# Experts of a mixture in plain fp32, weights stationary, instead of three reduced-precision products with the tokens stationary

## The reference, cut to what matters

```
logits = h @ w_router + b_router                 # 8 experts
probs  = softmax(logits); the two largest of each token are kept and normalised: gates
for e in range(8):
    y += gates[:, e] * ((silu(h @ w_gate[e]) * (h @ w_up[e])) @ w_down[e])
h = layer_norm(alpha * h + y)
```

## Time and profile before

| | us |
|---|---|
| median of 3 runs | 3124.86 (3122.19 to 3125.25) |
| the profiled execution's own time | 3119.76 |
| its span | 3117.9 |
| TensorE busy | 2736.0 (88%) |
| its weight loads busy | 2260.0 (72%) |
| VectorE busy | 2104.4 (67%) |
| ScalarE busy | 1550.2 (50%) |

### The profile page before, as it was taken

How to read it: one execution, slowest core, us unless ns; L and a number is a source line. 1 busy time by engine, 2 the same in 40 slices (tenths; PEclk the granted TensorE clock), 3 DMA queues, 4 the chain that set the end, 5 groups by cost and what they waited for, 6 DMA issues and landing times.

```text
span 3117.9 us, 50172 instructions
## 1 busy us (share of the span) xinstructions
PE 2736.0 (88%) x21428; PEld 2260.0 (72%) x21428; DVE 2104.4 (67%) x2999; ACT 1550.2 (50%) x2209; POOL 79.9 (3%) x93
## 2 busy tenths in 40 slices
PE   8787996759878799999999999997699988899987
PEld 8457996559866567676766667675697988897977
DVE  4655546784434588797979778796585865576864
ACT  4433432522111477676767667674336454446443
POOL 0000000030000000000000000000000011000011
PEclk9669997879987799898989899999799999999999
DMA  6113543200011798898979789895343454344542
GB/s 215 44 38 112 176 149 94 69 1 4 4 38 30 256 338 310 289 355 290 351 276 365 275 320 322 296 353 175 84 140 109 129 161 144 102 121 123 155 126 90
DMA packets 373442, 547.71 MB, mean 176 GB/s; under 512 B 24492, under 2 KB 187784, under 8 KB 372956
## 3 DMA queue, kind: packets, MB, share of 16 engines
q1 hardware_dynamic: 371228, 541.54, 51.2%
q0 software_dynamic: 1984, 2.89, 0.3%
HBM read 540.46 MB, written 1.05 MB: 174 GB/s over the span
## 4 chain that ended last, share of the span: by engine, by line
PE 71%; DVE 16%; ACT 6%; issue 3%; DMA 2%; POOL 1%; SPq 0%; DVEq 0%; POOLq 0%; ACTq 0%
PE PS L157 18%; PE PS L158 18%; PE PS L159 18%; DVE wl L304 4%; ACT wh L295 3%; PE PS L958 1%; PE PS L1689 1%; PE PS L372 1%; DMA raw<-in_w_in 1%; PE PS L1708 1%; PE PS L477 1%; PE PS L1716 1%; PE PS L986 1%; PE PS L2211 1%; PE PS L2183 1%
## 5 line engine op out<-in xcount | busy, mean ns | idle before, releaser
L304 DVE TENSOR_TENSOR wl<-raw,wh 128x1024 fp32r<-128x1024 f32 (+1 forms) x654 | 774.2, 1189 | 487.0 <-ACT wh L295 469.8
L295 ACT ACTIVATE wh<-raw 128x1024 fp32r<-128x1024 f32 (+1 forms) x654 | 670.6, 1027 | 669.9 <-PE PS L159 577.9
L304 DVE TENSOR_TENSOR wl<-more,wh 128x1024 fp32r<-128x1024 f32 x384 | 467.5, 1224 | 55.4 <-ACT wh L295 33.4
L295 ACT ACTIVATE wh<-more 128x1024 fp32r<-128x1024 f32 x384 | 406.8, 1060 | 141.9 <-PE PS L159 141.8
L157 PE MATMUL PS<-b_hn_h,wh 128*128 128x256 f32 (+2 forms) x1312 | 378.7, 289 | 26.3 <-DVE wl L304 10.8
L159 PE MATMUL PS<-b_hn_h,wl 128*128 128x256 f32 (+2 forms) x1312 | 371.1, 283 | 0.0
L158 PE MATMUL PS<-b_hn_l,wh 128*128 128x256 f32 (+2 forms) x1312 | 370.7, 283 | 0.0
L157 PE MATMUL PS<-wh,xe_h 128*96 128x512 f32 x896 | 358.0, 400 | 0.0
L158 PE MATMUL PS<-wl,xe_h 128*96 128x512 f32 x896 | 354.0, 395 | 0.0
L159 PE MATMUL PS<-wh,xe_l 128*96 128x512 f32 x896 | 351.1, 392 | 0.0
L157 PEld LDWEIGHTS PS<-b_hn_h,wh 128*128 128x128 f32 (+2 forms) x1312 | 232.1, 177 | 32.0 <-issue 16.9
(11 more groups left out here) (488 smaller groups left out, 5335.3 us busy)
## 6 DMA issues: line engine op xcount, KB each, us to landing
more<-in_moe_w_up SPq DMA_DIRECT2D x64, 1024.0 KB, 5.7
more<-in_moe_w_gate SPq DMA_DIRECT2D x64, 1024.0 KB, 5.5
more<-in_moe_w_down SPq DMA_DIRECT2D x64, 1024.0 KB, 5.5
raw<-in_w_in SPq DMA_DIRECT2D x56, 1024.0 KB
raw<-in_moe_w_gate SPq DMA_DIRECT2D x48, 1024.0 KB, 5.7
raw<-in_moe_w_up SPq DMA_DIRECT2D x48, 1024.0 KB, 5.3
raw<-in_moe_w_down SPq DMA_DIRECT2D x48, 1024.0 KB, 5.8
raw<-in_w_in SPq DMA_DIRECT2D x32, 704.0 KB
```

The source lines that it names most:

```text
L295: act.e.activation(st.two(n)[0], st.raw(n), ACT.Copy).then_inc(*act.sig("hi", st.name, n, sem=f"hi_{st.name}"))
L304: dve.e.tensor_tensor(lo, st.raw(n), hi.bitcast(F32), SUB).then_inc(*dve.sig("lo", st.name, n, sem=f"lo_{st.name}"))
```

## The change

- The three fp32r products and the split of the weights go. Each 128 x 128 tile of weights, as it was loaded, is the stationary operand of one plain fp32 matmul, and the 96 tokens of the expert move (`xe`, 128 x 96 for each of 8 feature tiles). The result has the hidden feature on the partitions, so `turned` goes too; the down product's result is transposed once (`turn`, 8 transposes an expert), scaled by the gate, split, and scattered with two fp32r products.
- The gather makes the transposed tokens directly (24 plain fp32 matmuls an expert, `Ht` stationary, `P1` moving); the picks of all experts are made at once, and the gates by slot by 24 small matmuls once.
- The weights lie in memory in the order in which the kernel reads them (`expert_tiles`, made before the launch): each load is 1 MB in one piece, 8 KB for each partition. Both sides read the same loads. A load is freed by the last matmul that uses it.
- There are 13 slots: six of them (EARLY) lie in memory that the layer before no longer uses from y_mean on, and SyncE issues six loads there right after the first three that follow bonus_v, ahead of the rest of rw_w_o and the router; three (RAW) and four (LATE, where wh and wl were) are used once the router's weights have been read. SyncE no longer waits for the flag.
- The high and low split of the transposed H goes; the rank is stored as rank + 1, and 0 for a token that isn't the expert's.

The diff, cut to its core (the dense side, which follows the same loads, and the constants are left out):

```diff
+    EARLY_AT = [u_at(3), u_at(5)] + [u_at(10) + n * 8192 for n in range(4)]
+    EARLY = [m_tile(f"early{n}", o, 2048) for n, o in enumerate(EARLY_AT)]
+    LATE = [m_tile(f"late{n}", PARTS_AT + n * 8192, 2048) for n in range(NPART)]
+    SM = Stream("M", EARLY + RAW + LATE, PARTS)
...
-    Ht = two("Ht", 3, D)
-    xe = [two(f"xe{n}", KC, CAP) for n in range(2)]
-    P1 = [tile3(f"P1{n}", 3, CAP, F32R) for n in range(2)]
-    G = tile("G", D)
-    PG = [tile(f"PG{n}", T) for n in range(2)]
-    hid = [tile(f"hid{n}", 512) for n in range(2)]
-    mh = two("mh", FE // 128, CAP)
...
+    Ht = tile3("Ht", 3, D)
+    P1 = tile("P1", 3 * NE * CAP).rearrange("p (i e r) -> p i e r", i=3, e=NE)
+    xe = [tile3(f"xe{n}", KC, CAP) for n in range(2)]
+    mt = [tile(f"mt{n}", 4 * CAP) for n in range(2)]
+    assert top[0] <= u_at(10)
+    top[0] = u_at(0)
+    mh = tile3("mh", NF, CAP)
+    Yh, Yl = tile("Yh", D, F32R), tile("Yl", D, F32R)
...
+            for j in range(2):
+                for x in range(2):
+                    SM.add(("in", e_, 2 * g + x, j), [(lambda sl: sl, A["moe_in"][e_, 2 * g + x, j])])
+        for n in range(KC * NF // 16):
+            SM.add(("out", e_, n), [(lambda sl: sl, A["moe_out"][e_, n])])
...
+    def load_moe(sp):
+        m = sp.piece["M"]
+        if m == 0:
+            sp.wait_ge(sp.at("y_mean"))
+        elif m == len(EARLY):
+            sp.wait_ge(sp.at("direct", "A", SA.of["router"]))
+        load(sp, SM)
...
+    def sparse_order(x, gather, project, down, turn, scatter):
+
+        gather(x, 0)
+        for e_ in range(NE):
+            project(x, e_, 0)
+            if e_:
+                turn(x, e_ - 1, 1)
+            project(x, e_, 1)
+            if e_:
+                scatter(x, e_ - 1)
+            for g in range(2, NG):
+                project(x, e_, g)
+            down(x, e_, range(0, 2))
+            if e_ + 1 < NE:
+                gather(x, e_ + 1)
+            down(x, e_, range(2, 6))
+            turn(x, e_, 0)
+            down(x, e_, range(6, 8))
+        turn(x, NE - 1, 1)
+        scatter(x, NE - 1)
...
     def sparse_pe(pe):
+        def gather(pe, e_):
+            pe.wait_ge(pe.at("picks"))
             for hf in range(2):
                 pe.wait_ge(pe.at("ht", 2, 1))
+                b = take("xe", e_, hf)
+                for k in range(4):
+                    f = 4 * hf + k
+                    for i, (q0, qn) in enumerate(QT):
+                        t = e.matmul(PS[:, b, k * CAP:(k + 1) * CAP], Ht[0:qn, i, f * 128:(f + 1) * 128], P1[0:qn, i, e_, :],
+                                     start=i == 0, stop=i == 2)
                 t.then_inc(*pe.sig("xe_mm", e_, hf))
             rows_pe(pe, "rank_row", e_, rt)
+            if e_ == 0:
+                b = take("slots")
+                for x in range(NE):
+                    for i, (q0, qn) in enumerate(QT):
+                        t = e.matmul(PS[0:CAP, b, x:x + 1], P1[0:qn, i, x, :], sc[i][0:qn, 56 + x:57 + x], start=i == 0,
+                                     stop=i == 2)
+                t.then_inc(*pe.sig("slots_mm"))
+
+        def project(pe, e_, g):
+            for j, what in enumerate(("gate", "up")):
+                pe.wait_ge(pe.at("xe", e_, 1))
+                b = take(what, "s", e_, g)
+                for x in range(2):
+                    m = SM.of["in", e_, 2 * g + x, j]
+                    w = pair_view(moe_load(pe, m))
+                    for y in range(2):
+                        o = (2 * x + y) * CAP
+                        for k in range(KC):
+                            t = e.matmul(PS[:, b, o:o + CAP], w[:, y, k, :], xe[e_ % 2][:, k, :], start=k == 0, stop=k == KC - 1)
+                    t.then_inc(*moe_used(pe, m))
+                pe.also(what + ".mm", "s", e_, g)
+
+        def down(pe, e_, rows):
+            for i in rows:
+                if i % 4 == 0:
+                    take("yt", e_, i // 4)
+                o = i % 4 * CAP
+                for f in range(NF):
+                    c = i * NF + f
+                    m = SM.of["out", e_, c // 16]
+                    w = row_view(moe_load(pe, m))
+                    pe.wait_ge(pe.at("up", "s", e_, f // 4))
+                    t = e.matmul(PS[:, bank_of["yt", e_, i // 4], o:o + CAP], w[:, c % 16, :], mh[:, f, :], start=f == 0,
+                                 stop=f == NF - 1)
+                    if c % 16 == 15:
+                        t.then_inc(*moe_used(pe, m))
+                if i % 4 == 3:
+                    pe.also("yt.mm", e_, i // 4)
+
+        def turn(pe, e_, half):
+            pe.wait_ge(pe.at("yt", e_, half))
+            b = take("y", e_, half)
+            for i in range(4):
+                o = (4 * half + i) * CAP
+                t = e.transpose(PS[0:CAP, b, i * 128:(i + 1) * 128], YT[:, o:o + CAP], ident)
+            t.then_inc(*pe.sig("turn_mm", e_, half))
+
+        def scatter(pe, e_):
             pe.wait_ge(pe.at("rank_row", "s", e_))
             for f in range(KC):
+                pe.wait_ge(pe.at("y_lo", e_, f // 4))
+                b = take("scattered", e_, f)
+                c = slice(f * 128, (f + 1) * 128)
+                e.matmul(PS[:, b, 0:T], Yh[:, c], PG[e_ % 2], start=True, stop=False)
+                e.matmul(PS[:, b, 0:T], Yl[:, c], PG[e_ % 2], start=False, stop=True).then_inc(*pe.sig("scattered_mm", e_, f))
+
+        sparse_order(pe, gather, project, down, turn, scatter)
...
-                    for k1 in range(0, KC, 2):
-                        n, (wh, wl) = piece(pe, SM)
-                        for k in range(2):
-                            t = mm3(e, PS[0:CAP, b, :], xh[:, k1 + k, :], xl[:, k1 + k, :], wh[:, k, :], wl[:, k, :],
-                                    k1 + k == 0, k1 + k == KC - 1)
-                        t.then_inc(*used(pe, SM, n))
...
     def sparse_act(act):
+        def project(act, e_, g):
+            act.wait_ge(act.at("gate.mm", "s", e_, g))
+            if g >= 2:
+                act.wait_ge(act.at("up", "s", e_, g - 2))
+            elif e_:
+                act.wait_ge(act.at("up", "s", e_ - 1, NG - 1 if g % 2 == (NG - 1) % 2 else NG - 2))
+            e.activation(mt[g % 2], ps("gate", "s", e_, g, n=4 * CAP), ACT.Silu).then_inc(*act.sig("gate", "s", e_, g))
+
+        def turn(act, e_, half):
+            act.wait_ge(act.at("turn_mm", e_, half))
+            act.wait_ge(act.at("slots"))
             if e_:
+                act.wait_ge(act.at("scattered_mm", e_ - 1, KC - 1))
+            e.activation(Yh[0:CAP, half * 512:(half + 1) * 512], ps("y", e_, half, p=CAP, n=512), ACT.Copy,
+                         scale=gs[0:CAP, e_:e_ + 1]).then_inc(*act.sig("y_hi", e_, half))
...
     def sparse_dve(dve):
+        def project(dve, e_, g):
+            dve.wait_ge(dve.at("gate", "s", e_, g))
+            dve.wait_ge(dve.at("up.mm", "s", e_, g))
+            if e_:
+                dve.wait_ge(dve.at("yt.mm", e_ - 1, 1))
+            e.tensor_tensor(flat(mh[:, 4 * g:4 * g + 4, :]), mt[g % 2], ps("up", "s", e_, g, n=4 * CAP), MUL).then_inc(
+                *dve.sig("up", "s", e_, g))
+
+        def down(dve, e_, rows):
+            if rows[0] == 0:
+                return
+            half = 0 if rows[0] == 2 else 1
+            dve.wait_ge(dve.at("yt.mm", e_, half))
+            if e_:
+                dve.wait_ge(dve.at("turn_mm", e_ - 1, half))
+            e.tensor_copy(YT[:, half * 4 * CAP:(half + 1) * 4 * CAP], ps("yt", e_, half, n=4 * CAP)).then_inc(
+                *dve.sig("yt", e_, half))
+
+        def turn(dve, e_, half):
+            dve.wait_ge(dve.at("y_hi", e_, half))
+            c = slice(half * 512, (half + 1) * 512)
+            e.scalar_tensor_tensor(Yl[0:CAP, c], ps("y", e_, half, p=CAP, n=512), gs[0:CAP, e_:e_ + 1],
+                                   Yh[0:CAP, c].bitcast(F32), MUL, SUB).then_inc(*dve.sig("y_lo", e_, half))
+            dve.also("y", e_, half)
...
+        e.memset(Yh[CAP:128].bitcast(F32), 0.0)
+        e.memset(Yl[CAP:128].bitcast(F32), 0.0)
+        for i, (q0, qn) in enumerate(QT):
+            t = e.tensor_tensor(P1[0:qn, i], bc(iota_r[0:qn], [qn, NE, CAP], 1), bc(rk[i][0:qn], [qn, NE, CAP], 2), ALU.is_equal)
+        t.then_inc(*dve.sig("picks"))
+        sparse_order(dve, gather, project, down, turn, scatter)
...
-            for hf in range(2):
-                c = slice(hf * 512, (hf + 1) * 512)
-                dve.wait_ge(dve.at("ht_hi", i, hf))
-                e.tensor_tensor(Ht[1][0:qn, i, c], ps("ht", i, hf, p=qn, n=512), Ht[0][0:qn, i, c].bitcast(F32), SUB).then_inc(
-                    *dve.sig("ht", i, hf))
-        for i, (q0, qn) in enumerate(QT):
             dve.wait_ge(dve.at("rank_mm", i))
-            e.tensor_copy(rk[i][0:qn], ps("rank", i, p=qn, n=8)).then_inc(*dve.sig("rank", i))
+            e.scalar_tensor_tensor(rk[i][0:qn], ps("rank", i, p=qn, n=8), 1.0, mk[i][0:qn], ADD, MUL).then_inc(
+                *dve.sig("rank", i))
```

(54 more changed lines are left out.)

266 lines of the change are left out of this document (74 added, 192 removed).

## The result

The changed kernel takes 3289.23 us (median of 4 runs, 3285.77 to 3291.14), the kernel before 3123.53 beside it (3120.52 to 3125.25). The ratio is 1.0527, 95% interval 1.0514 to 1.054: slower by 165.7 us. Predicted were 3285 us, between 3238 and 3315, and slower with 0.93. The profiled execution took 3289.37, its span is 3287.4.

The account below looks back on a forecast made before the run. TensorE was taken to bound the experts' stage. 1046 + 1204 + 41 + 7 + 14 + 7.2 = 2319 for its end, 162 us later than 2156.87; so 3282 profiled, 3285 predicted, range 3238 to 3315.

Parts of the forecast that it names:

- The price of a pass: Main matmuls: each plain fp32 pass costs its weight load of 128 columns, 0.112 us; 10752 passes, 1204 us against 927.
- Rival (a): Main matmuls: loads hide and the moving side bounds, 0.081 us a pass, 871 us, total 2952, faster; 5 in 100.
- From the first main pass to the last: Experts' stage: main passes 1204 us, seven more gathers 41, turns 7, scatters 14.
- The start: Experts' stage up to its first main pass: that pass at about 1046 instead of 1054.49, 8.5 us gained.
- The branch: Ahead of the experts' memsets and picks: 3.5 us for the branch, on the other engines too.
- the slots' matmuls: 24 small matmuls for the gates by slot, before the first main pass: 4.0 to 7.8 us, taken as 4.5.
- The tail: End of the experts' stage, from the last pass through scatter and adds: 7.2 us, where it was 5.3.
- The splits are worth nothing by themselves: Experts' stage: the weight splits are off the path, so removing them gains nothing by itself.
- The loads hide: Expert weight loads: 44.04 MB an expert in about 159 us, 277 GB/s, stay hidden; 0 us added.
- The clock: TensorE in the experts' stage: granted clock near 1.00 where it was 0.94, since the seam no longer idles.
- rival (b): TensorE's clock falls to 0.50 for the whole experts' stage, 4414, or only at each expert's seam, 3353; 5 in 100.

## Why the prediction was right, step by step

**The price of a pass** was the step that decided, and it was exact: 0.112 predicted; measured 0.1115 in the last 112 passes, and the same within 0.001 in every group of one expert's window. The rows that it came from were a handful of loads elsewhere in the kernel. The runs with 64, 48 and 128 columns show that it is the load's and not the moving side's: it falls with the columns loaded, and at a given clock it stays when those moved are halved or grow by a third. Rival (a), the four matmuls of line 1716, showed a true spacing (0.084 where the load is short), of the side that does not bound.

**From the first main pass to the last**: predicted 1204 + 41 + 7 + 14 = 1266 us; measured 1057.28 to 2323.33, 1266.0. That the two agree so closely is partly chance: at the 0.1117 that is the mean of one expert's window the passes come to 1201, 3 less than 1204, and small things not in the sum (17 passes at half clock, gathers of 6.0) make up for it.

**The start** was mis-sized: 1046 predicted (the terms themselves add up to 1045.4), 1057.28 measured, 11.3 us, where the range allowed 5. 2.6 of it is where the stage began; executions with the same code ahead of it differ by 6.2 there (1008.67 and 1014.86, above), so this is no effect of the change that a run shows. The branch took 6.75 (0.55 + 0.10 + 6.10) where I had 3.5, because of the loads that the change itself puts beside it (3.48 for the 6.10 where they are held back). The gather took 10.55 where I had 8, the rank row 1.20 for 0.5, the slots' matmuls 7.77 for 4.5: all three ran at clock 0.50 to their end, the upper ends of the bounds given (10.4 and 7.8), where I had chosen the middle for the gather and a value near full clock for the slots' matmuls. The memsets, 2.0, and the picks, 2.7, were right. So the 8.5 us that the start was to gain came to nothing (46.3 for 46.1).

**The tail** took 5.8, not 7.2. After the stage the changed kernel needs 958.3 us, the one before 961.0; I had assumed them equal. With the same code there, the runs on the changed kernel lie between 956.4 and 961.0 and those on the kernel before between 961.0 and 965.1; why is not shown. The errors (+11.3, -1.4, -2.7) leave 3289.3 for the profiled execution against 3282. That the median came within 4 us of 3285 is partly luck: errors of opposite sign, and 3 us added for a distance between median and profiled execution that the changed kernel does not have (3289.23 and 3289.37).

**The splits are worth nothing by themselves**: right inside the stage, not at its start. In the kernel with the gather alone VectorE still makes them all, at 113.92 of 129.60 us, and TensorE is busy for 129.36. But the first high part and two low parts (1.07 and 2.36 us) stand ahead of the picks in the chain there, and putting the picks first was worth 11.4 us.

**The loads hide**: right, 278 GB/s; the DMA share in an expert is 0.81, just above the 0.8 that was named as its bound. No run shows a cost or a gain of the early loads. The layout, priced at zero, measured 1.0002.

**What the prediction did not split**: it set 927 us of main products against 1204, as one price. The runs divide it, in this order: the new gather -65, plain fp32 in place of three fp32r products +208, all the rest of the change +22, together +165 of the 165.7. Inside the stage (from the router's first matmul to the layer norm's adds) the same steps are -68.6, +209.1 and +29.1 in the profiled executions; the time outside it varies by 8 us between them, so the last step is known to some 7 us only. An expert's products take 168 x 0.69 = 115.9 us in three fp32r matmuls, 168 x 0.858 = 144.1 in plain fp32 with the tokens stationary, and 1344 x 0.1115 = 149.9 with the weights stationary; over eight experts that is 226 for the first step and 46 for the second. The first earns 11 back at the start (46.2 to 35.0). The second earns part of it back in each expert: the period grows by 2.3 us (156.8 to 159.1) instead of 5.8, since the hidden part needs no transposes (28 in each expert with the tokens stationary, 2.3 us) and the scatter uses fp32r (2.05 us for 3.67). That makes 18 us for the swap of sides over eight experts; the other 11 of the 29.1 are the longer start (35.0 to 46.3).

**The clock**: "I expect the opposite" was right for the stage (1.00 where it was 0.94), but the argument against rival (b) was thinner than its 5 in 100 suggests. It rested on 8 columns moved against 96; the run with 48 shows the fall of clock half way between, and its 4409 us are what rival (b) had priced (4414).

## What to carry to other kernels

Price a matmul by the larger of its two sides, at its own pass count: columns loaded and columns moved, each from a row of the same clock. Taking work off an engine that does not bound (here 105 us of VectorE in each expert) buys nothing where the two run side by side, and what it adds to TensorE's passes is paid in full; look in the profile at the busy time of weight loads beside that of matmuls. A change of many parts can hold a good one: test them one by one before dropping the whole.

## What the runs showed of the hardware

- Plain fp32 takes two passes whichever side is stationary: 0.429 us a pass with 512 columns moving, 0.1115 with 128 loaded and 96 or 128 moving, 0.083 to 0.084 with 64 loaded and 96 moving.
- A TensorE that is busy all the time can still be granted clock 0.50: with 128 columns loaded and 48 moved it stayed there for most of some 2400 us, and came back to 1.00 for moments behind matmuls of 272 columns.
- A branch costs 3.1 to 3.5 us until VectorE's first instruction with idle DMA engines, and 5.6 to 6.5 where weight loads fill them (six runs; holding the loads back took it from 6.10 to 3.48).
- Contiguous 1 MB loads lower the DMA engines' busy share (0.88 to 0.83 at 315 GB/s, 0.95 to 0.90 at 340) without a change in time where TensorE bounds.
